# Attention in a hybrid S5 / RG-LRU / mLSTM block: blocks that both directions share are multiplied by the values once

## The reference

```
s   = einsum(qc, kc) * exp(dmat - m_t)
num = s @ vc + sc * (qc @ cmat)
den = sum(s) + sc * (qc @ nvec)
h   = num / maximum(abs(den), exp(-m_t))
```

## Time and profile before

| | |
|---|---|
| median of 3 runs | 2739.13 us |
| profiled execution, its own time | 2739.68 us |
| its span | 2738.1 us |
| PE, DVE, ACT, POOL busy | 94%, 56%, 30%, 36% of the span |
| mean granted TensorE clock | 0.975 of full speed |

### The profile page before, as it was taken

One profiled execution on the slowest core, in us unless ns is written; L12 is line 12 of the kernel. 1 busy time (PEld: TensorE's weight loads), 2 busy tenths in 40 slices (PEclk: granted clock), 3 DMA queues, 4 the chain that ended last, 5 costly groups with the idle time before them and its releaser, 6 DMA issues.

```text
span 2738.1 us, 37623 instructions
## 1 busy us (share of the span) xinstructions
PE 2567.0 (94%) x13319; PEld 1986.8 (73%) x13319; DVE 1532.6 (56%) x2362; ACT 829.4 (30%) x997; POOL 980.3 (36%) x1163
## 2 busy tenths in 40 slices
PE   7897889989998998989998999999999999999998
PEld 2786755445444666878886877778989989898787
DVE  4677755888866224442327656775555664656510
ACT  2425634361643113221212111212323242422210
POOL 0139967887800000011133333444433433341000
PEclk9999999999999999999998999999999999999999
DMA  8312320101105777441114333565132321314421
GB/s 299 109 59 99 106 76 24 58 23 50 43 23 175 241 227 234 100 185 44 35 47 103 133 118 108 173 207 211 35 110 75 104 76 34 123 47 163 138 92 46
DMA packets 257472, 298.09 MB, mean 109 GB/s; under 512 B 34960, under 2 KB 217528, under 8 KB 256960
## 3 DMA queue, kind: packets, MB, share of 16 engines
q1 hardware_dynamic: 201568, 206.60, 23.9%
q10 hardware_dynamic: 51168, 73.04, 7.5%
q0 software_dynamic: 4608, 16.78, 1.8%
HBM read 203.09 MB, written 93.29 MB: 108 GB/s over the span
## 4 chain that ended last, share of the span: by engine, by line
PE 71%; DVE 9%; ACT 3%; issue 2%; DMA 1%; POOL 0%; ACTq 0%; DVEq 0%; SPq 0%; POOLq 0%
PE ps L135 63%; PE ps L1317 6%; DVE xc_part L2447 1%; ACT L1512 1%; PE ps L973 1%; ACT arena L1512 1%; PE ps L1322 0%; PE ps L1250 0%; DVE arena L520 0%; DVE arena L2375 0%; PE ps L1149 0%; DVE wo_full L2460 0%; DVE arena L2211 0%; DVE wo_part L2447 0%; DVE s_scan_tmp L2159 0%
## 5 line engine op out<-in xcount | busy, mean ns | idle before, releaser
L135 PE MATMUL ps<-h_full,weights 128*128 128x512 f32 (+1 forms) x1152 | 427.5, 532 | 26.0 <-ACT arena L1512 8.4
L135 PE MATMUL ps<-h_part,in_weight_parts 128*128 128x512 f32 (+1 forms) x1920 | 414.5, 377 | 14.2 <-DVE arena L2364 6.7
L135 PEld LDWEIGHTS ps<-h_part,in_weight_parts 128*128 128x128 f32 x1920 | 338.1, 191 | 85.9 <-issue 13.7
L135 PEld LDWEIGHTS ps<-h_full,weights 128*128 128x128 f32 x1152 | 221.8, 194 | 225.2 <-issue 206.2
L135 PE MATMUL ps<-v_part,p_part 128*128 128x512 f32 x1248 | 294.9, 395 | 0.1
L135 PEld LDWEIGHTS ps<-v_part,p_part 128*128 128x128 f32 x1248 | 234.1, 190 | 49.1 <-issue 0.8
L135 PE MATMUL ps<-q_part,xc_part 128*128 128x256 f32 x1920 | 244.7, 286 | 3.9 <-DVE q_part L2480 3.9
L135 PEld LDWEIGHTS ps<-q_part,xc_part 128*128 128x128 f32 x1920 | 234.5, 192 | 4.8 <-DVE q_part L2480 4.5
L135 PE MATMUL ps<-arena,weights 64*16 64x128 f32 (+2 forms) x896 | 177.6, 394 | 15.3 <-ACT arena L1512 14.4
L1317 PE MATMUL ps<-wo_part,mx_part 128*128 128x512 f32 x768 | 183.8, 400 | 5.0 <-DVE mx_part L2447 4.6
L2787 POOL TENSOR_TENSOR in_weight_parts<-weights,ones 128x1024 fp32r<-128x1024 f32 x32 | 81.0, 2532 | 264.4 <-PE ps L135 189.5
(11 more groups left out here) (398 smaller groups left out, 4193.6 us busy)
## 6 DMA issues: line engine op xcount, KB each, us to landing
weights<-in_e_w_in SPq DMA_DIRECT2D x32, 512.0 KB, 4.3
weights<-in_o_w_in SPq DMA_DIRECT2D x32, 512.0 KB, 4.5
s_out_maps<-arena ACTq DMA_DIRECT2D x16, 640.0 KB, 2.9
arena<-s_out_maps SPq DMA_DIRECT2D x16, 640.0 KB, 4.8
ml_xcv<-arena ACTq DMA_DIRECT2D x16, 640.0 KB, 3.0
xc_full<-ml_xcv SPq DMA_DIRECT2D x4, 2560.0 KB, 9.0
xm_tiles<-ml_xm SPq DMA_DIRECT2D x16, 640.0 KB, 3.8
weights<-in_mod_w POOLq DMA_DIRECT2D x17, 512.0 KB, 4.9
```

Source lines behind the costliest of these rows:

```text
L135: return nc.tensor.matmul(o, lhsT, rhs, start=(k == 0), stop=(k == n - 1))
```

## The change

For a query row, the context pair and the diagonal pair hold source blocks that both directions read. The weights of direction 1 (backward) are multiplied by the ratio of the two clipped denominators (forward over backward) and added to the weights of direction 0 (forward); then only this sum is multiplied with the values, and the result is divided by the forward denominator alone. For that the denominators are needed as rows along the queries, before the values are multiplied:

- `row_sums(i, q)` on PE: all-ones by `Sp`, an f32 matmul of 128x128 by 512 columns, which puts both denominators of 256 queries on all partitions. It takes a place ("d", q) in `SLOTS`. The list says where: for q = 0 after the scores (1, 1), for 1 and 2 after the first scores of query block q + 1, for 3 inside `weighted(2)`, between its halves.
- `row_step(q, n)` on VectorE, eight instructions: n = 0, maximum with exp(-m) and with the negated sum (512 columns each); n = 1, reciprocal of 256 columns and a product of 256; n = 2, for the context pair, a product and a sum of 512 columns; n = 3, for the diagonal pair, a product and a sum of 256.
- exp(-m) is stored to memory by ScalarE once and read back by SP, spread over all partitions, `em_rows_in`: two transfers of 256 columns for each head and query block.
- The splits of pairs 0 and q + 1 (`shared_high`, `shared_low`) come after these steps, and have 512 and 640 columns in place of 1024 and 768. `value_sums` starts with the six blocks of the other pairs (18 matmuls) and waits for the shared ones only then; it has 30 matmuls in place of 39.
- `sum_up` keeps its number of additions and columns. The buffers `PH` shrink to 21 times 128 columns. In `head_out(3, 1)` only the forward bank is left.

```diff
             SLOTS += [("v", p + 1), ("s", 0, p)]
         SLOTS += [("q", 2, 0), ("q", 2, 1)]
         for p in range(NPR):
-            SLOTS += [("v", p + 6), ("s", 1, p)]
-        SLOTS += [("v", 11), ("q", 3, 0), ("q", 3, 1)] + [("s", q, p) for q in (2, 3) for p in range(NPR)]
+            SLOTS += [("v", p + 6), ("s", 1, p)] + [("d", 0)] * (p == 1)
+        SLOTS += [("v", 11), ("q", 3, 0), ("q", 3, 1)]
+        for q in (2, 3):
+            for p in range(NPR):
+                SLOTS += [("s", q, p)] + [("d", q - 1)] * (p == 0)
+        SLOTS += [("d", 3)]
...
-                return [(I, d, 0, QW) for I in range(2) for d in range(2)]
+                return [(I, d, 0, QW) for I in range(2) for d in (1, 0)]
             if 2 * p == J0:
-                return [(J0, 0, 0, QW), (J0 + 1, 1, 0, QW), (J0 + 1, 0, P, P), (J0, 1, 0, P)]
+                return [(J0, 1, 0, P), (J0 + 1, 1, 0, QW), (J0, 0, 0, QW), (J0 + 1, 0, P, P)]
             return [(I, int(I > J0), 0, QW) for I in (2 * p, 2 * p + 1)]
...
-        def sources(q, j, d):
-
-            J = CBLK + 2 * q + j
-            return [I for I in range(NBLK) if I < CBLK or (I <= J if d == 0 else I >= J)]
+        def shared_pair(q, p):
+            return p == 0 or 2 * p == CBLK + 2 * q
...
+        SPLITS = [(0, 2), (0, 3), (0, 4), (1, 1), (1, 3), (1, 4), (0, 0), (0, 1), (2, 1), (2, 2), (2, 4), (1, 0), (1, 2),
+                  (3, 1), (3, 2), (3, 3), (2, 0), (2, 3), (3, 0), (3, 4)]
+        SPLIT_N = {x: n + 1 for n, x in enumerate(SPLITS)}
+
+        def splits_done(q, shared):
+            return max(SPLIT_N[q, p] for p in range(NPR) if shared_pair(q, p) == shared)
+
+        def sources(q, j):
+
+            J0 = CBLK + 2 * q
+            J = J0 + j
+            early = [(I, 0) for I in range(CBLK, J0)] + [(I, 1) for I in range(J0 + 2, NBLK)]
+            late = [(J0, 0) if j else (J0 + 1, 1)] + [(J, 0), (0, 0), (1, 0)]
+            return early, late
...
+            def em_rows_in(i, q):
+                if not (isinstance(i, int) and i == 0 and q < 2):
+                    sp.wait_ge(*past("ps_ready", 8 * i + (2 * q - 2)))
+                for d in range(2):
+                    o = QW * (1 - d)
+                    sp.dma_start(EB[:, q % 2, o:o + QW], em_row(i + MH * d, q)).then_inc(sem(f"em_in{q % 2}"), 16)
...
+                em_rows_in(i, 2)
                 after_mixed(i, 0)
-                sp.wait_ge(*past("lo_mm", LO * i + LO))
+                em_rows_in(i, 3)
+                sp.wait_ge(*past("lo_mm", slot_done(i, "s", 3, NPR - 1)))
                 if not last:
                     column_rows_in(i + 1)
                     map_rows_in(i + 1)
                     sp.wait_ge(*past("p_ready", 20 * i + 20))
                     decay_rows(i + 1)
+                    em_rows_in(i + 1, 0)
...
+            def row_sums(i, q):
+
+                pe.wait_ge(*past("sums", 36 * i + (9 * q + 9)))
+                mm(slot(i, "d", q), ones[:, :], Sp[:, q % 2], 0, 1).then_inc(sem("lo_mm"), 1)
+
             def value_sums(i, q, j):
                 u0 = isinstance(i, int) and i == 0 and q == 0
                 if j == 0:
-                    pe.wait_ge(*past("pl_ready", 20 * i + (5 * q + 5)))
+                    pe.wait_ge(*past("pl_ready", 20 * i + splits_done(q, False)))
                 if q == 0 and j == 0:
-                    pe.wait_ge(*past("vq_ev", 20 * i + EVICTED["v", 11]))
+                    pe.wait_ge(*past("vq_ev", NEV * i + EVICTED["v", 11]))
                 if u0 and j == 0:
                     pe.wait_ge(*past("z_ev", MT))
                 if not u0:
                     pe.wait_ge(*past("h_ev", 8 * i + (2 * q + j - 1)))
-                for d in range(2):
-                    Is = sources(q, j, d)
-                    for n, I in enumerate(Is):
-                        c = PIECE_AT[q][I, d] + P * j
-                        for m, (a, b) in enumerate(PARTS):
-                            mm(ps[:, 2 + 2 * j + d], Ps[a][:, q % 2, c:c + P], Vs_[b][:, I], 3 * n + m, 3 * len(Is))
+                early, late = sources(q, j)
+                total = [sum(y[1] == d for y in early + late) for d in range(2)]
+                done = [0, 0]
+                for n, (I, d) in enumerate(early + late):
+                    if j == 0 and n == len(early):
+                        pe.wait_ge(*past("pl_ready", 20 * i + splits_done(q, True)))
+                    for m, (a, b) in enumerate(PARTS):
+                        c = (HIGH_AT, PIECE_AT)[a][q][I, d] + P * j
+                        mm(ps[:, 2 + 2 * j + d], Ps[a][:, q % 2, c:c + P], Vs_[b][:, I], 3 * done[d] + m, 3 * total[d])
+                    done[d] += 1
...
+                    if q == 2 and j == 0:
+                        row_sums(i, 3)
...
+                    if p == 1:
+                        row_sums(i, 0)
...
+                        if p == 0:
+                            row_sums(i, q - 1)
...
+            def shared_high(i, q):
+                for p in (0, q + 1):
+                    weights_high(i, q, p)
...
                 def weights_low(q, p):
-                    a, b = PAIR_AT[q][p]
-                    dve.wait_ge(*past("ph_ready", 20 * i + (5 * q + p + 1)))
-                    dve.wait_ge(*past("sums", 36 * i + (9 * q + 2 * p + 1)))
-                    low(PL[:, q % 2, a:b], PR[:, q % 2, a:b], PH[:, q % 2, a:b], "pl_ready")
+                    splits.append((q, p))
+                    dve.wait_ge(*past("ph_ready", 20 * i + SPLIT_N[q, p]))
+                    dve.wait_ge(*past("sums", 36 * i + (9 * q + (9 if shared_pair(q, p) else 2 * p + 1))))
+                    low(whole_pair(PL, q, p), whole_pair(PR, q, p), split_pair(PH, HIGH_PAIR, q, p), "pl_ready")
+
+                def shared_low(q):
+                    for p in (0, q + 1):
+                        weights_low(q, p)
+
+                def row_step(q, n):
+
+                    z = q % 2
+                    E = EB[:, z]
+                    r0, r1 = E[:, QW:2 * QW], E[:, 0:QW]
+                    if n == 0:
+                        dve.wait_ge(*past(f"em_in{z}", 64 * i + (32 * (q // 2) + 32)))
+                        dve.wait_ge(*past("lo_mm", slot_done(i, "d", q)))
+                        den = slot_bank("d", q)
+                        rlink(V.tensor_tensor(E, den, E, ALU.max))
+                        V.scalar_tensor_tensor(out=E, in0=den, scalar=-1.0, in1=E, op0=ALU.mult, op1=ALU.max).then_inc(sem("vq_ev"), 1)
+                        dve.wait_ge(*past("vq_ev", NEV * i + EVICTED["d", q]))
+                    elif n == 1:
+                        rlink(V.reciprocal(r1, r1))
+                        rlink(V.tensor_tensor(r0, r0, r1, ALU.mult))
+                    elif n == 2:
+                        a, b = PAIR_AT[q][0]
+                        x = PR[:, z, a:b].rearrange("p (i d c) -> p i d c", i=2, d=2)
+                        rlink(V.tensor_tensor(x[:, :, 0], x[:, :, 0], r0.unsqueeze(1).to_broadcast([P, 2, QW]), ALU.mult))
+                        V.tensor_tensor(x[:, :, 1], x[:, :, 1], x[:, :, 0], ALU.add).then_inc(sem("ps_ready"), 1)
+                    else:
+                        a, b = PAIR_AT[q][q + 1]
+                        x = PR[:, z, a:b].rearrange("p (h b c) -> p h b c", h=2, b=3)
+                        u, v = x[:, 0, 0::2], x[:, 1, 0::2]
+                        rlink(V.tensor_tensor(u, u, r0.rearrange("p (j c) -> p j c", j=2), ALU.mult))
+                        V.tensor_tensor(v, v, u, ALU.add).then_inc(sem("ps_ready"), 1)
...
-                    if p:
+                    if p and not shared_pair(q, p - 1):
...
+                    if p:
+                        row_step(0, p - 1)
                 value_low(11)
                 for h in range(2):
                     query_low(i, 3, h)
                 weights_low(1, NPR - 1)
+                shared_low(0)
...
                     for p in range(NPR):
                         weigh(q + 2, p)
+                        if p < 4:
+                            row_step(q + 1, p)
                         if p in (2, 4):
                             mixed(i, q, p // 2 - 1)
-                    weights_low(q + 2, NPR - 1)
+                    if not shared_pair(q + 2, NPR - 1):
+                        weights_low(q + 2, NPR - 1)
+                    shared_low(q + 1)
+                for n in range(4):
+                    row_step(3, n)
                 head_out(2, 0)
+                shared_low(3)
...
```

More of the change, by code:

```diff
@@ L385, in build @@
         EVICTED = {x: sum(y[0] != "s" for y in SLOTS[:n + 1]) for n, x in enumerate(SLOTS)}
+        TAKEN = {x: sum(y[0] in "vq" for y in SLOTS[:n + 1]) for n, x in enumerate(SLOTS)}
+        NEV = EVICTED["d", 3]
         LOB = (0, 1, 7)
-        assert LO == 40 and [x for x in SLOTS if x[0] == "s"] == [("s", q, p) for q in range(NQ) for p in range(NPR)]
+        assert LO == 44 and NEV == 24 and [x for x in SLOTS if x[0] == "s"] == [("s", q, p) for q in range(NQ) for p in range(NPR)]
         def slot_bank(*x):
```

(22 more changed lines are left out.)

83 lines of the change are left out of this document (63 added, 20 removed).

## The result

The changed kernel took 2782.71 us (median of 4 runs, 2777.45 to 2787.66), the kernel before 2739.24 us (2737.72 to 2740.1) beside it. The ratio is 1.0163, 95% interval 1.0144 to 1.0182: slower, as forecast, but 22.7 us above the forecast of 2760 us and 8.7 us above the upper end of the range.

What follows compares the result with a forecast made beforehand. PE was taken to set the pace, with VectorE's list deciding at some waits. From 2739.1 us, 9 us net lost across the heads gave 2748, and 12 us of slower clock gave 2760 us; range 2740 to 2774.

Steps and rivals of the forecast that it cites:

- PE sheds and takes: PE in attention: 288 fewer matmuls save 67.5 us, 16 row sums cost 13.9 us, net 53.6 us saved.
- What VectorE takes: VectorE in attention: row_step 6.0 us for each q, splits about 0.65 us less; net 86 us more.
- rival 1: VectorE's new two-buffer instructions hold up GpSimd, mainly delaying weighted(1): 13 us a pass, 2773 us; chance 0.15.
- Place A: weighted(0): starts 2.2 us later, but 18 fewer matmuls give 4.2 back; 2.0 us won a head.
- Place B: weighted(1): after the early matmuls PE waits 3.3 us for the shared splits; 0 won.
- Place C: weighted(2) and head's end: PE waits 1.9 us, then columns come late behind q = 3 steps; 9.0 us lost, three times.
- Place D: From value_sums(3, 0) to value_sums(3, 1): 18 fewer matmuls, little waiting touched; 4.2 us won.
- The last head: No queries follow; VectorE's chain sets the end: 2.8 us lost, 2.0 won, so 0.8 us lost.
- The clock: PE's clock falls after waits in weighted(1), weighted(2) and at head ends: 12 us, between 0 and 20.
- Rival 2: PE's clock does not fall in the short waits, the sum stands alone: 2748 us; chance 0.18.
- Rival 3: PE remains the bound, VectorE arriving in time: 2733 us in the milder form, 2685 us with all waits gone; chance 0.12.

Runs made afterwards that it cites:

- pool_light: Changed kernel with GpSimd's additions of pairs 1 to 4 cut to 16 columns each (denominators wrong): 2743.15 us.
- halves_end: Changed kernel with the orders of halves and end_order taken together: 2733.80 us, ratio 0.9980 to the kernel before.
- fill: Changed kernel with 182 useless matmuls added in PE's long waits so that PE is not idle there: 2770.11 us.
- halves: Changed kernel with PE taking the early matmuls of both halves of each weighted(q) before the late ones, row sums of q = 3 between: 2743.69 us.
- end_order: Changed kernel with only step n = 0 of q = 3 before the next head's columns on VectorE, ScalarE's shared parts moved likewise: 2772.09 us.
- columns_first: halves_end with the next head's map and four column instructions also ahead of head_out(2, 0) on VectorE and ScalarE: 2734.87 us.

## Why the prediction was right in its direction and short by 23 us

**PE sheds and takes: right but for 2.5 us.** 960 matmuls, as forecast. The 0.2345 us a matmul is 9.14 / 39 with the tail still in it, though the prediction says it was taken off. From start to next start 39 take 8.95 us (2450.48 to 2459.43 in the trace before) and 30 take 6.92 (2116.45 to 2123.37 in the trace after): 2.03 us less, not 2.11, in all 65.0 us and not 67.5. A row sum moves what follows it by 0.86 us (2100.34 to 2101.20), as forecast; the 16.7 us of its group count the overlap with the next matmuls too. Of the 4.6 us that are neither clock nor idle time the other 2.1 stay unexplained.

**What VectorE takes: too little, and only beside GpSimd.** The reciprocal was right (1.746 us against 1.75), so the estimate of 2.3 us from the repeat count in the Trainium skill (VectorE: DVE Perf Modes, section on the 8-slice pipeline) is not what this chip took. The four two-buffer instructions were put at 2.6 us a q with the splits' row as measure. They took 0.97 + 1.01 + 0.96 + 0.74 = 3.7 us, and a whole `row_step` 7.5 us instead of 6.0. The timeline shows such instructions beside GpSimd's additions and, at the head's end, without them:

```profile
2142.85 0.68 DVE L2553 TENSOR_TENSOR p_part<-p_full,p_part 128x512 fp32r<-128x512 f32 x1
...
2143.09 2.19 POOL L3028 TENSOR_TENSOR decays<-decays,p_full 128x256 f32<-128x256 f32 x2 [1.56 <-DVE p_full L2699]
2143.45 1.23 DVE L2670 TENSOR_TENSOR p_full<-p_full,em_rows 128x512 f32<-128x512 f32 x1
...
2147.64 2.47 POOL L3028 TENSOR_TENSOR decays<-decays,p_full 128x512 f32<-128x512 f32 x2 [2.37 <-DVE p_full L2697]
2148.01 1.51 DVE L2676 TENSOR_TENSOR p_full<-p_full,em_rows 128x256 f32<-128x256 f32 x1
...
2203.45 0.69 DVE L2670 TENSOR_TENSOR p_full<-p_full,em_rows 128x512 f32<-128x512 f32 x1
...
2204.78 0.42 DVE L2676 TENSOR_TENSOR p_full<-p_full,em_rows 128x256 f32<-128x256 f32 x1
```

1.23 against 0.69 and 1.51 against 0.42 us. This is the mechanism of rival 1, which I had let work in one direction only, VectorE holding up GpSimd. GpSimd's 256-column additions took 953 ns on average, less than the 1090 in the earlier trace rows, and VectorE paid most. In these rows it is the later starter that is drawn out: the split that began 0.24 us ahead of GpSimd's additions kept its 0.68 us, and the products that began behind them took 1.23 and 1.51. GpSimd paid too, with 2.19 us for two additions here and 1.55 for the two that ran beside the reciprocal (2139.97). The Trainium skill (SBUF — State Buffer, section on the two sides) speaks of one exclusive lock for either engine; these rows agree that the two exclude each other. pool_light shows it by experiment: with the additions cut, 966 and 962 ns became 774 and 484.

**Place A: one of the two microseconds.** `weighted(0)` started 22.84 us after the first score instead of 21.9; start of q = 1 to start of q = 2 is 37.43 us (2093.61 to 2131.04) where it was 38.43: 1.0 won, forecast 2.0.

**Place B: forecast 0, measured 3.6 lost** (2131.04 to 2168.54 is 37.50 us, before 33.92). The early matmuls started at 16.1 as forecast; the wait was 4.35 us instead of 3.3, and 2.15 us went to the clock right behind it.

**Place C and the head's end: forecast 9.0 lost, measured 12.4** (from the first score of q = 3 to `value_sums(3, 0)` 48.62 us, before 36.22). The cause is the one forecast. The wait was 4.06 instead of 1.9 us and the fall behind it cost 2.3, so VectorE's chain began at 31.2 (2199.75) instead of 26.25. It then took 16.5 us to the end of the columns instead of 18.5. `row_step` was 5.9 us there, as forecast; nearly all of the difference is the four column splits:

```profile
2196.98 4.47 POOL L3004 TENSOR_TENSOR decays<-xb_rows,att_small 128x128 f32<-128x128 f32 x8 [3.71 <-DMA xb_rows<-ml_rows]
```

```profile
2210.60 5.69 DVE L2553 TENSOR_TENSOR xc_part<-xc_full,xc_part 128x1280 fp32r<-128x1280 f32 x4
```

5.69 us in place of 7.32. In the kernel before, eight GpSimd instructions of that kind (2183.30 to 2193.10) ran beside the splits; here GpSimd was done 9 us before them. In halves_end, where they run side by side again (2173.78 to 2182.47 and 2176.52 to 2183.82), the four take 7.30 us. So it is the mechanism of rival 1 once more, this time in the change's favour. The idle time of PE at the queries, 6.4 us a head, is therefore less than my 9, though the start is later.

**Place D: 3.4 of 4.2 won**: start to start 11.99 us against 13.37, and 7.09 against 9.11 for the second.

**The last head: forecast 0.8 lost, measured 9.0** (from the first score of q = 1 to the output projection 140.79 us, before 131.78). A won 1.1 us, B lost 2.7, and from the first score of q = 3 on 7.4 were lost instead of 2.8, with a wait of 3.62 us in C, a fall behind it (5.49 us for twelve) and 4.56 us of waiting at `transposed(2, 0)`. From the first score of q = 1 to that of the next head, the first three heads lost 10.3, 11.6 and 16.3 us; the places above follow the second.

**The clock is the step that failed.** In the attention stretch the forecast was 62.6 us more of idle time and 12 us of clock; the trace has 65.1 and 31.2. These 19.2 us, the 2.5 of idle time and the 4.6 that are neither are the 26 us by which the stretch grew more than forecast. That the sum of the waits was right within 3 us is luck: `row_step` was put 1.5 us too short on average, which made the waits in B and C longer, and the column splits 1.6 us too long, which made those at the head's end shorter. The 12 us of clock were three falls of 2 us at the heads' ends and five falls among the eight waits of B and C, 6 us. All eight of those waits were followed by a fall, and they cost 17.0 us: the six of heads 1 to 3 between 1.6 and 2.5 us each (4.60 to 5.49 us for what takes 3.04), 13.1 together, and the two of the last head 3.9. So both the count and the price were too low. The waits themselves were 3.6 to 4.35 us and not the 1.9 and 3.3 of the forecast. The rest fell at the heads' ends and where no long wait stands just ahead, as the 8.70 us for 30 matmuls after 1.77 us of waiting in the third head. By the medians the whole loss is 43.5 us and not 47.3; which term is smaller there no trace shows. fill confirms the kind of cost: take the idleness away and leave the lateness, and 12.6 us come back.

**Rival 2** (no falls) is out: the windows after the waits stand at 0.54 and 0.57, near the 1.2 GHz level of 0.50, and that over the queries of the head's end at 0.74. **Rival 3** did not come by itself, but its conditions were right: when the two orders are taken together, halves against the waits in B and C and end_order against the one at the head's end, PE is nearer to being the bound and the kernel is slightly faster than before. Rival 3's 2733 us asked only for B and C; halves did that and gave 2743.69, mostly for the clock: 17.0 us more were lost to it than in the kernel before, where the rival had 6. It fell at the head's end (8.91 us for 30) and in `value_sums(3, 1)` (8.66 to 8.72 us for 30 in each of the three heads).

Of what was to show it: the reciprocal, the count of matmuls and the cause of the waits at the queries came true, these waits with 6.4 us in place of some 9; the waits in B and C ended at or just above the 2 to 4 us given; 227 us for the 960 matmuls (255.6), PE busy at 560 (591.0), a clock of 0.97 (0.93) and 20 us for the stretch (47.3) did not.

**What stays open.** halves_end has 14.4 us more of busy time than 555.2 (8.0 us more than before are lost to the clock in it, added up in slices as above) and 31.9 us more idle time than before; 53.6 less 46.3 is what it wins in its profiled run (7.3 us; 4.6 against the before of that comparison by the medians, 2738.44). Which orders of VectorE's list at the head's end would win the rest was tried once only (columns_first).

## What to carry to other kernels

Work taken from the busiest engine can be worth less than nothing if it is handed to the engine whose list that one waits for: compare, at each wait, when both lists arrive, with the new work in its place. The order in which the work is asked for is then worth nearly as much as the new work itself: the same instructions gave 2782.71 and 2733.80 us, and making `row_step` nearly free in the old order gave 2729.19. Give a wait of PE that has grown to some 4 us the price of a fall of the clock besides, here 4.35 + 2.15 us, while the eight waits of 0.83 to 1.30 us in pool_light had none; and give a two-buffer instruction beside GpSimd its slow price.

## What the runs showed of the hardware

- VectorE's two-buffer instructions beside GpSimd's additions: 512 columns 1.23 instead of 0.69 us, 256 columns 1.51 instead of 0.42; four splits of 1280 columns 7.3 us beside other GpSimd instructions, 5.69 without. One that started just ahead of GpSimd's kept its time (0.68 us). Instructions that read PSUM kept theirs (L2661 of `row_step`, 685 ns in both kernels with full and with cut additions).
- After equal waits the clock fell or did not: 3.46 us of waiting, then twelve matmuls in 3.06 or in 5.49 us, in two heads of one execution.
- A reciprocal of 256 columns took 1.746 us, in line with 64 and 1280 columns.
- One kernel's runs spread by more than the differences asked for here: columns_first 2728.85 to 2740.95 us over 12 runs, the kernel before 2733.02 to 2741.65 over the 17 beside it. The 4.6 us of halves_end rest on ten runs and an interval, not on one profile.
